# Two-block transformer in fp32: block 2's mixer projected by token, a joint norm factor at the join, and an earlier fold

## What is computed

```
h = rmsnorm(h, final_norm)                      # end of block 1
for i in range(2):                              # block 2
    a = rmsnorm_2(h, norm_mix_pre[i]);  u = a @ w_in[i]
    q, k, v, qi, ki, wi, u_conv, u_pool = split(u)   # 512, 128, 128, 1024, 64, 16, 512, 256
    q, k, qi, ki = partial rope (16 of 64 columns of each head)
    idx[t, s] = sum over 16 heads of wi[t, head] * relu(qi[t, head] . ki[s])
    y_attn = attention of 8 heads over the 64 keys of each token that idx ranks highest
    y_conv = silu(layernorm(conv 31 taps of a*sigmoid(g))) @ conv_pw
    y_pool = (means over 2, 4, 8, 16 tokens - u_pool) @ pool_w * pool_scale
    h = h + rmsnorm_2(concat(y_attn, y_conv, y_pool) @ w_out[i], norm_mix_post[i])
    h = h + rmsnorm_2(square(relu(rmsnorm_2(h) @ w_up)) @ w_down)
    h = h + sigmoid(h @ ple_gate[i]) * (p[i] @ ple_proj[i])
```

## Time and profile before

| what | value |
|---|---|
| median of 3 runs | 2159.07 us (2158.53 to 2161.93) |
| profiled execution, its own time | 2161.07 us |
| its span, mean granted TensorE clock | 2159.3 us, 0.946 |
| busy: TensorE, VectorE, ScalarE, GpSimd | 91%, 66%, 47%, 10% |
| block 2 layer 0: gate of block 1 ends, w_out ends | 1258.9 and 1480.4 us |
| block 2 layer 1: gate of layer 0 ends, w_out ends | 1712.8 and 1919.5 us |

### The profile page before, as it was taken

The page is one execution under the profiler, slowest core; times in us unless marked ns, Lnnn a source line. Parts: engine busy times, 40 slices in busy tenths (PEclk is TensorE's granted clock), DMA queues, the critical chain, the costliest instruction groups (busy, mean ns, idle before and its releaser), DMA issues.

```text
span 2159.3 us, 36568 instructions
## 1 busy us (share of the span) xinstructions
PE 1972.7 (91%) x15880; PEld 1946.1 (90%) x15880; DVE 1417.2 (66%) x1676; ACT 1010.4 (47%) x1226; POOL 214.4 (10%) x148
## 2 busy tenths in 40 slices
PE   7999999999989999999999977658999886489998
PEld 7999999999989999999999967648999876489998
DVE  6656776755575556877655567874655778846556
ACT  5434455543464444455534446543443555534333
POOL 2001000100020001000100014501000136010000
PEclk9999999999999999999999988768999987689999
DMA  7555455455545555444555533112555431134552
GB/s 261 176 193 166 136 185 166 156 195 187 184 142 188 184 187 186 142 147 153 193 192 179 179 102 107 50 59 98 178 194 195 143 103 59 42 110 170 176 186 79
DMA packets 254724, 331.00 MB, mean 153 GB/s; under 512 B 6246, under 2 KB 229028, under 8 KB 254564
## 3 DMA queue, kind: packets, MB, share of 16 engines
q1 hardware_dynamic: 254210, 328.23, 45.9%
q10 hardware_dynamic: 258, 0.16, 0.0%
q0 software_dynamic: 96, 0.26, 0.0%
HBM read 327.58 MB, written 1.05 MB: 152 GB/s over the span
## 4 chain that ended last, share of the span: by engine, by line
PE 72%; DVE 16%; ACT 6%; POOL 3%; issue 2%; DMA 1%; POOLq 0%; ACTq 0%; DVEq 0%; SPq 0%
PE work L1871 16%; PE work L1872 16%; PE work L1873 16%; PE acc L1873 7%; PE acc L1871 7%; PE acc L1872 7%; DVE w_lo L1217 4%; ACT w_hi L760 2%; POOL fa L690 2%; DVE fa L1651 2%; POOL fa L717 1%; DVE fa L1262 1%; ACT fa L1032 1%; DVE rstd L1256 1%; DVE ra L1230 1%
## 5 line engine op out<-in xcount | busy, mean ns | idle before, releaser
L1871 PE MATMUL work<-xh,w_hi 128*128 128x256 f32 x2928 | 841.2, 287 | 36.7 <-DVE xl L1251 20.5
L1872 PE MATMUL work<-xl,w_hi 128*128 128x256 f32 x2928 | 836.4, 286 | 0.0
L1873 PE MATMUL work<-xh,w_lo 128*128 128x256 f32 x2928 | 834.1, 285 | 0.0
L1217 DVE TENSOR_TENSOR w_lo<-raw,w_hi 128x2048 fp32r<-128x2048 f32 (+1 forms) x314 | 709.6, 2270 | 116.7 <-ACT w_hi L760 114.7
L760 ACT ACTIVATE w_hi<-raw 128x2048 fp32r<-128x2048 f32 (+1 forms) x314 | 580.7, 1855 | 170.2 <-PE work L1873 86.2
L1871 PEld LDWEIGHTS work<-xh,w_hi 128*128 128x128 f32 x2928 | 568.1, 194 | 42.7 <-issue 30.6
L1872 PEld LDWEIGHTS work<-xl,w_hi 128*128 128x128 f32 x2928 | 568.7, 194 | 0.5
L1873 PEld LDWEIGHTS work<-xh,w_lo 128*128 128x128 f32 x2928 | 568.0, 194 | 0.0
L1262 DVE TENSOR_TENSOR fa<-work,rstd 128x512 f32<-128x512 f32 x182 | 124.8, 689 | 414.0 <-PE work L1873 413.2
L1871 PE MATMUL acc<-ra,w_hi 128*128 128x256 f32 x1344 | 377.4, 281 | 2.8 <-DVE ra L1230 2.8
L1873 PE MATMUL acc<-ra,w_lo 128*128 128x256 f32 x1344 | 377.4, 281 | 0.0
(11 more groups left out here) (236 smaller groups left out, 1847.7 us busy)
## 6 DMA issues: line engine op xcount, KB each, us to landing
raw<-in_ffn_w_gu_dram SPq DMA_DIRECT2D x88, 1024.0 KB, 5.1
raw<-in_w_in_dram SPq DMA_DIRECT2D x56, 1024.0 KB, 5.4
raw<-in_ffn_w_down_dram SPq DMA_DIRECT2D x44, 1024.0 KB, 5.1
raw<-in_w_up_dram SPq DMA_DIRECT2D x32, 1024.0 KB, 5.5
raw<-in_w_down_dram SPq DMA_DIRECT2D x32, 1024.0 KB, 6.9
raw<-in_w_mla_out_dram SPq DMA_DIRECT2D x8, 1024.0 KB, 5.5
raw<-in_w_o_dram SPq DMA_DIRECT2D x8, 1024.0 KB, 5.4
raw<-in_w_ple_gate_dram SPq DMA_DIRECT2D x8, 1024.0 KB, 5.3
```

Source lines behind the costliest of these rows:

```text
L1217: v.tensor_tensor(w_lo[:, s, 0:n], raw[:, r, 0:n], w_hi[:, s, 0:n].bitcast(F32), ALU.subtract).then_inc(lo_done.sem, 1)
L1871: pe.matmul(dst, ah, bh, start=start and i == 0, stop=False, skip_group_check=not group)
L1872: pe.matmul(dst, ah, bl, start=False, stop=False, skip_group_check=not group)
L1873: last = pe.matmul(dst, al, bh, start=False, stop=stop and i == len(pairs) - 1, skip_group_check=not group)
```

## The change

1. **Joint factor.** Block 2 layer 0 takes `xh`, `xl` and the squares straight from the un-normalised `h` as each bank leaves block 1's last gate: `joint[0:8]` is `final_norm` times the pre-norm gain, `joint[8:16]` the root of `final_norm`² + eps, which makes the pre-norm's sum the one that both norms need. `h` itself is normalised later (`final_norm()`), in VectorE's list behind the second index projection, with a second fold, sum and root of its own.
2. **First stage.** `ki`, `wi` and the last four index heads are one 336-column slab in two chunks (6 and 2 k-tiles); both token halves of it and the convolution's `a` are made in one loop over k, behind a wait for all three chunks. The sum of squares follows it, also by token (`cols`).
3. **By token.** Index queries, keys, values and queries are projected with tokens on partitions; rope is done in PSUM on the 16 columns of each head, ScalarE scales the rows out, and TensorE turns them (`turned`). The rotation matmuls and one of two splits go.
4. **Index products first.** `dots` go to `acc` banks 1 to 3, relu is done in place, `weighted` reads PSUM. Keys, queries and pool are projected during TopK; three tap buffers instead of two.
5. **Outputs by token.** The exponentials go to TensorE unnormalised; each head's output is scaled by ScalarE on its way out and turned at the end. The convolution's norm, the pool branch and `pw` come behind the heads.
6. **w_out by rows**: four chunks of 256 input rows, accumulated in `acc`, the first three as soon as their rows are there.
7. **Fold order.** GpSimd's fold waits for `xl` tile 5 instead of 7, or for none (block 1's norm 0 of layer 1, block 2's norm 0). In block 1 the gate's third projection is put around the last output product (`halves`). `unit_taken` becomes four semaphores.

```diff
+    out = [("w_in_2", 0, 6, IN2_QI + 768, 336), ("w_in_2", 6 * P, 2, IN2_QI + 768, 336)]
+    out += [("w_in_2", 0, KD, at, 256) for at in (IN2_A, IN2_G, IN2_QI, IN2_QI + 256, IN2_QI + 512, IN2_KV,
+                                                 IN2_Q, IN2_Q + 256, IN2_P)]
+    out += [("w_out_2", row, 2, 0, D) for row in (0, 256)]
     out += [("conv_pw_2", 0, 2, 0, 256)]
-    out += [("w_out_2", 0, KD, i * 256, 256) for i in range(4)]
...
-                    gp.wait_ge(xl_ready.sem, xl_ready.after(here, behind * KD + KD - 1))
+                    gp.wait_ge(xl_ready.sem, xl_ready.after(here, behind))
...
-                fold(here, 0, 0, 0)
-                fold(here, 1, NB, 1)
-                fold(here, 2, 2 * NB + 1, 2)
-                fold(here, 3, 3 * NB + 1, 3)
+                fold(here, 0, 0, None if layer else KD - 1)
+                fold(here, 1, NB, 1 * KD + 5)
+                fold(here, 2, 2 * NB + 1, 2 * KD + 5)
+                fold(here, 3, 3 * NB + 1, 3 * KD + 5)
...
-                        act.wait_ge(h_new.sem, h_new.after((15, 0), b - NB))
-                        act.activation(sq[:, 2 * b:2 * b + 2, :], h[:, 2 * b:2 * b + 2, :], ACT.Square).then_inc(sq_ready.sem, 1)
+                        act.wait_ge(h_new.sem, h_new.after(mid, b - NB))
+                        for k in (2 * b, 2 * b + 1):
+                            act.activation(xh[:, k, :], h[:, k, :], ACT.Copy, scale=joint[:, k:k + 1]).then_inc(xh_ready.sem, 1)
+                        act.wait_ge(joint_ready, 1)
+                        for k in (2 * b, 2 * b + 1):
+                            last = act.activation(sq[:, k, :], h[:, k, :], ACT.Square, scale=joint[:, 8 + k:9 + k])
+                        last.then_inc(sq_ready.sem, 1)
...
+                for c in range(1, 4):
+                    two_taps()
+                    rows_of(("qi", c), c, c % 2)
+                    two_taps()
+                    relus(c - 1)
+                    if c == 1 and layer == 0:
+                        make_std(here, "pre")
+                    index_queries(c)
+                    two_taps()
+                    next_hi(here, QI2[c])
                 two_taps()
...
 (VectorE)
+                def rope(view, heads, name):
+
+                    n = (P, TB, heads, 16)
+                    a, b = (x[:, 0:TB * heads * 16].rearrange("p (a b n) -> p a b n", a=TB, b=heads) for x in (rope_a, rope_b))
+                    cos, sin = (rope_cs[:, i, :, :].rearrange("p (a o) n -> p a o n", o=1) for i in range(2))
+                    v.tensor_tensor(a, view[:, :, :, 0:16], cos.to_broadcast(n), ALU.mult)
+                    v.tensor_tensor(b[:, :, :, 0:8], view[:, :, :, 8:16], sin[:, :, :, 0:8].to_broadcast([P, TB, heads, 8]), ALU.mult)
+                    chain(here, v.tensor_tensor(b[:, :, :, 8:16], view[:, :, :, 0:8],
+                                                sin[:, :, :, 8:16].to_broadcast([P, TB, heads, 8]), ALU.mult))
...
+                def final_norm():
+
+                    v.wait_ge(std_ready.sem, std_ready.after(here, "pre"))
+                    v.reciprocal(rstd[:, 1, :], std[:, 0, :]).then_inc(rstd_ready.event(here, "pre"), 1)
+                    v.wait_ge(rstd_ready.sem, rstd_ready.after(here, "pre"))
+                    for b in range(NB):
+                        for k in (2 * b, 2 * b + 1):
+                            last = v.scalar_tensor_tensor(h[:, k, :], h[:, k, :], column((1, 1), V1_FINAL + k),
+                                                          rstd[:, 1, :], ALU.mult, ALU.mult)
+                        last.then_inc(h_new.sem, 1)
...
+                def weighted(c):
+
+                    v.wait_ge(*relu_done.at(here, 3 * c + 2))
+                    for g in range(4):
+                        hd = INDEX_HEADS[c] + g
+                        late, early = acc[:, 1 + g // 2, g % 2 * T:g % 2 * T + T], acc[:, 3, g * P:g * P + P]
+                        parts = ((1, idx[:, P:384], late), (0, idx[:, 0:P], early))
+                        for tb, dst, src in parts:
+                            if (c, g) == (0, 0):
+                                last = v.tensor_scalar(dst, src, wi[:, tb, hd:hd + 1], None, ALU.mult)
+                            else:
+                                last = v.scalar_tensor_tensor(dst, src, wi[:, tb, hd:hd + 1], dst, ALU.mult, ALU.add)
+                        chain(here, last)
...
+                    if r == 3:
+                        next_lo(here, KV2)
...
 (TensorE)
+                w = [weights(here, c) for c in (QK2, QK2 + 1, A2)]
+                for k in range(KD):
+                    pe.wait_ge(*xl_ready.at(here, k))
                     for tb in range(TB):
-                        last = flip(bank(u)[:, tb * P:tb * P + P], xr[:, p, tile, tb * P:tb * P + P])
+                        last = product(bank(U2["qk", tb])[:, 0:336], [(tiles((xh, xl), everything, k, slice(tb * P, tb * P + P)),
+                                                                       columns(w[k // 6], k % 6 * 336, 336))],
+                                       start=k == 0, stop=k == KD - 1, group=False)
+                        if k == KD - 1:
+                            last.then_inc(unit_ready.sem, 1)
+                    for m in range(2):
+                        last = product(bank2(U2["a"])[:, m, :], [(columns(w[2], k * 256 + m * P), tiles((xh, xl), everything, k, everything))],
+                                       start=k == 0 and m == 0, stop=k == KD - 1, group=False)
+                    if k == KD - 1:
+                        last.then_inc(unit_ready.sem, 1)
...
+                pe.wait_ge(*dot_taken.at(here, 11))
+                pe.wait_ge(*unit_taken.at(here, U2["ota"]))
+                accumulate(here, WO2[0], rows(0), first=True)
+                pe.wait_ge(*unit_taken.at(here, U2["out", HEADS - 1]))
+                turned("otb", ot[1])
...
+                accumulate(here, WO2[1], rows(2))
+                pe.wait_ge(*part_lo.at(here, "ly"))
+                project(here, PW2, U2["pw"], depth=2, x=(lyh, lyl))
+                for k in range(2):
+                    pe.wait_ge(*unit_taken.at(here, U2["poolw", k]))
+                accumulate(here, WO2[2], rows(6))
+                pe.wait_ge(*unit_taken.at(here, U2["pw"]))
+                accumulate(here, WO2[3], rows(4), done=0)
...
-                project(here, c, UE["gc", 2])
-                output(PAIRS - 1)
-                pe.wait_ge(unit_taken.sem, unit_taken.after(here, UE["o", PAIRS - 1]))
+                halves(here, c, UE["gc", 2], lambda: output(PAIRS - 1))
```

More of the change, by code:

```diff
@@ L1962, in accumulate @@
                                        [(columns(w, k * D + (2 * b + a) * P), tiles(x, everything, k, everything))
-                                        for k in range(2)], start=False, stop=done is not None, group=False)
+                                        for k in range(2)], start=first and a == 0, stop=done is not None, group=False)
                     if done is not None:
@@ L2235, in scores @@
+                turned(("qt", 1), tm[:, 1, :, :])
                 def scores(hd):
```

975 lines of the change are left out of this document (516 added, 459 removed).

## The result

The changed kernel takes 2071.51 us, the median of 4 runs (2069.38 to 2073.7), against 2159.26 of the kernel before: ratio 0.9592, 95% interval 0.9575 to 0.9608. Forecast were 2074. The profiled execution took 2069.59 us, span 2067.8, 91.5 less than the one before, where the sum said 85.

A forecast was written before the change was run, and what follows sets the result against it. Block 2's mixer was taken as bound by VectorE's order of work, not matmuls. Layer 1 −34, layer 0 −35, folds −13 and `halves` −2.8 sum to −85: 2076 us, median 2074; forecast case 2058 to 2094, wider range 2040 to 2114.

The forecast's parts named there:

- The start: Block 2's first product: 12.7 us after the gate in layer 0, 8.0 in layer 1, after the third chunk's split.
- The index cycle: Block 2's index stage: 11.8 us per group of four heads, ScalarE the bound; layer 1's stage ends at 85.7, not 126.1.
- TopK and w_out: Block 2, layer 1: TopK 19.5 us instead of 13.2, w_out 27.0 instead of 25.6.
- Attention: Block 2, layer 1, up to the first w_out product: 35.8 us instead of 41.8, nearest to VectorE's work and engine hops.
- The final norm: Layer 0's index stage: `final_norm` in VectorE's list and a root on ScalarE add 7.3 us.
- The haircut: Block 2's mixers: gain cut by 4.7 us in layer 1 and 5 in layer 0 for semaphore delays and port contention.
- The folds: TensorE's waits for GpSimd's fold: starting two `xl` tiles earlier gives −13 us, bounds 0 and 14.
- `halves`: Block 1's gate projection: covers a wait of 1.4 us in each layer, −2.8 us (0 to 2.8).
- GpSimd as the pace of the taps: Slower rival, index stage: GpSimd's tap adds at 3.6 us set the cycle, about 2172 us; chance 0.04.
- TensorE at half clock through the whole mixer: No-change rival, block 2's mixer: some 912 matmuls at 0.213 us each, about 2157 us; chance 0.03.
- The case of more gain: Rival: TensorE bounds the index cycle at 9.4 us and attention at full clock gives 10 more, 2045 us; chance 0.14.
- half the gain: Rival, index stage: slow `weighted` from PSUM and interlocks on `acc` banks make cycles 14.8 us, 2094 to 2114; chance 0.24.

## Why the prediction was right, point by point

- **The start.** 14.3 and 8.7 us for 12.7 and 8.0; one weight split sets it, as said. Taking its wait away is worth 26 us over both layers, more than its length, which the forecast didn't count.
- **The index cycle.** 11.4 us for 11.8. `weighted` from PSUM, the one price no row showed, was put at 3.2 between 2.3 and 7.1, and is 3.1. The run with SBUF inputs gives the upper bound back. The bound itself was wrong: it is a loop through ScalarE and VectorE, and ScalarE, forecast without idle, idles 2.0 us in it. That the list summed to nearly the loop's length is luck. So is the end of the stage: in layer 1 the first index product came at 37.7 us for 41, and the three cycles and the last sum took 47.9 for 44.7; the two errors cancel in 85.6 for 85.7.
- **TopK and w_out.** 19.7 and 27.5 for 19.5 and 27.0.
- **Attention.** 37.1 for 35.8, near in size by luck: I derived it from VectorE's busy time, and it is TensorE at half clock. VectorE is busy 25 of 37 us. TensorE at 0.5 between TopK and w_out was on my own list of what would show the forecast wrong, and it came.
- **The final norm.** 8.5 us of TensorE's wait for 7.3. From the first index product to the last weighted sum layer 0 takes 54.2 us, layer 1 without the norm 47.8, so 6.4 by that measure.
- **The haircut.** 4.7 and 5 us for hops and contention weren't needed in the profiled execution: 169.9 against 168.0, and 181.4 against 181.3. The mixers gave 76.9 for 69, the rest 14.6 for 15.8, and so the sum of 85 was 6.5 short. For layer 0 this execution was a good one: in the profile with halving undone its w_out ends 186.0 us after the gate, nearly the sum with the 5.
- **The folds.** −13 against 12.4 by the run that undoes them, of which the waits show 10.8.
- **`halves`.** −2.8 against nothing: I costed the wait that went and not the weight split that the later gate unit holds up (2.05 us for 1.41).
- **The rivals.** GpSimd as the pace of the taps did not come as a loss: its adds took 1.29 us in the median, and the later cycles don't pass through them. But eight of the 60 took 2.6 to 3.1 us, each beside a weight split, which was another of the signs of being wrong, and with the rope moved they do set the pace. TensorE at half clock through the whole mixer came for attention alone (0.58; index stage 0.93). The rule of the Trainium skill on transposes ("TensorE: Matmul & The Clock Gate", Part 4: PE-mode transpose) points the right way there. The runs show more than it says: the same turns run at full clock in most runs when 48 more matmuls stand between them. The case of more gain, TensorE as the bound, did not come in the index stage; half the gain did not either.

Not tried: the joint factor undone alone, whose price is only known with the wait for the third chunk on top of it.

## What to carry to other kernels

Cost a moved step by what stands behind it in each engine's list: a weight split ahead of a first product, or one behind a gate unit that comes 1.4 us later, costs as much as a wait that was removed. Where VectorE's short operations run beside GpSimd, put one of their two inputs in PSUM; it is worth a factor of two to three here. When a stage shows TensorE busy and at half clock, it may gain by doing more: try it, over several runs. And before a difference between two profiles is put down to an edit, see whether it lies in a stage that the edit touches.

## What the runs showed of the hardware

- VectorE's scalar_tensor_tensor with two SBUF inputs beside GpSimd's adds: 1.498 us against 0.476 beside an idle GpSimd and 0.472 with one input in PSUM (128 x 256, medians). The weighted sums: 1.082 against 0.484. A weight split (128 x 2048) keeps 2.3 us, and the add beside it takes 2.6 to 3.4 us instead of 1.29.
- At half clock a matmul of 64, one of 128 and one of 256 columns cost about the same from one start to the next, 0.21 us; nine of 64 took 1.96 us, nine of 128 took 2.01.
- TensorE busy 29.7 of 30.1 us with short matmuls and turns stayed at 0.53 of its clock, that is, at 1.2 GHz for nearly all of it. With 48 matmuls of 256 columns more the stage was 26.6 instead of 30.1 us long, at 0.94. So here being busy went with half clock, and more matmuls with full clock, but not surely: with the wait left in, it fell and stayed at 0.54 for 26 us in which TensorE was busy throughout, fillers and all, and in layer 1 of that run it was at 0.50 for 22 us without such a wait. What decides between the two isn't settled.
